# Stick-breaking attention in groups of four heads, and its side projection moved to the delta stage

## The reference

```python
def stick_breaking(q, k, v, q_pos, k_pos):
    z = einsum('bqhd,bkhd->bhqk', q, k) * HEAD_DIM ** -0.5
    visible = k_pos[None, :] < q_pos[:, None]
    log_keep = where(visible, log_sigmoid(-z), 0.0)
    later = cumsum(log_keep, axis=3, reverse=True) - log_keep
    w = where(visible, exp(log_sigmoid(z) + later), 0.0)
    return einsum('bhqk,bkhd->bqhd', w, v)

def mixer_output(h, o_a, o_b, o_c, z, g_post, w_out):
    o = concatenate([o_a, o_b, o_c], axis=-1) * silu(z)
    return h + rmsnorm(einsum('btm,md->btd', o, w_out), g_post)
```

## Time and profile before

| | us |
|---|---|
| runs, median (lowest to highest) | 2085.74 (2085.29 to 2086.71) |
| profiled execution, span of the page | 2087.2 |
| PE busy | 1956.1 |
| DVE busy | 824.0 |
| ACT busy | 759.4 |
| POOL busy | 499.1 |

### The profile page before, as it was taken

How to read it: one execution, slowest core, us unless ns; L and a number is a source line. 1 busy time by engine, 2 the same in 40 slices (tenths; PEclk the granted TensorE clock), 3 DMA queues, 4 the chain that set the end, 5 groups by cost and what they waited for, 6 DMA issues and landing times. The chain is left out here.

```text
span 2087.2 us, 25680 instructions
## 1 busy us (share of the span) xinstructions
PE 1956.1 (94%) x9682; PEld 1222.7 (59%) x9682; DVE 824.0 (39%) x1596; ACT 759.4 (36%) x1590; POOL 499.1 (24%) x436
## 2 busy tenths in 40 slices
PE   6989993999999999999989998999999999969997
PEld 6944441666666666666645554555555555647775
DVE  5723432223222222222216775444454444553332
ACT  4413541222222222222214443344344444455564
POOL 0004312123222231223100000233332333324433
PEclk9999996999999999999998998999999999989999
DMA  4210204100000111102001112000100000165562
GB/s 127 95 32 10 65 1 27 32 27 32 21 32 27 62 57 37 32 27 67 21 28 45 41 41 73 11 21 17 61 28 11 21 7 11 39 180 155 168 191 89
DMA packets 120887, 108.13 MB, mean 52 GB/s; under 512 B 34337, under 2 KB 96065, under 8 KB 120769
## 3 DMA queue, kind: packets, MB, share of 16 engines
q1 hardware_dynamic: 117616, 95.62, 16.5%
q0 software_dynamic: 3152, 10.91, 1.4%
HBM read 65.54 MB, written 41.08 MB: 51 GB/s over the span
## 5 line engine op out<-in xcount | busy, mean ns | idle before, releaser
L330 PE MATMUL side_acc<-hT,wslot 128*128 128x512 f32 (+1 forms) x1360 | 592.5, 546 | 4.4 <-DMA wslot<-in_w_in 4.4
L1570 DVE TENSOR_TENSOR_SCAN prod<-keepb,prod 128x512 f32<-128x512 f32 (+4 forms) x184 | 208.4, 1133 | 286.8 <-ACT keepb L1509 286.4
L1552 POOL TENSOR_TENSOR beta<-beta,prod 128x512 f32<-128x512 f32 (+4 forms) x184 | 174.9, 951 | 588.0 <-DVE prod L1570 588.0
L330 PEld LDWEIGHTS side_acc<-hT,wslot 128*128 128x128 f32 x1360 | 218.3, 192 | 146.0 <-issue 135.6
L1509 ACT ACTIVATE keepb<-b_z 128x512 f32<-128x512 f32 (+4 forms) x184 | 97.7, 531 | 298.4 <-PE b_z L1443 191.2
L460 PE MATMUL acc<-hT,wslot 128*128 128x512 f32 (+1 forms) x480 | 180.6, 532 | 5.4 <-DMA wslot<-in_w_in 5.4
L1440 PE MATMUL b_z<-reg 64*128 64x512 f32 (+3 forms) x360 | 179.9, 580 | 4.8 <-PEq L1793 4.8
L724 POOL TENSOR_TENSOR atl<-at,cf 128x512 f32<-128x512 f32 x102 | 139.8, 1404 | 173.0 <-DVE at L944 173.0
L964 DVE TENSOR_TENSOR xt<-xt,b_kq 128x512 f32<-128x512 f32 x85 | 58.4, 688 | 303.5 <-PE b_kq L791 303.5
L1467 PE MATMUL b_o<-wt,vrow 128*64 128x128 f32 x1232 | 173.4, 280 | 0.5 <-DVE wt L1584 0.5
L1467 PEld LDWEIGHTS b_o<-wt,vrow 128*64 128x64 f32 x1232 | 129.5, 136 | 35.2 <-issue 33.7
(11 more groups left out here) (197 smaller groups left out, 2773.6 us busy)
## 6 DMA issues: line engine op xcount, KB each, us to landing
uT_scratch<-side_stage SPq DMA_DIRECT2D x36, 256.0 KB, 2.0
hT<-mix_scratch SPq DMA_DIRECT2D x17, 512.0 KB, 6.7
hT<-sz_scratch SPq DMA_DIRECT2D x17, 512.0 KB, 8.1
sz_scratch<-side_stage SPq DMA_DIRECT2D x32, 256.0 KB, 2.0
reg<-in_x_prompt SPq DMA_DIRECT2D x15, 512.0 KB
wslot<-in_w_in SPq DMA_DIRECT2D x15, 512.0 KB, 4.0
xres<-in_x_prompt SPq DMA_DIRECT2D x15, 512.0 KB
out_y_prompt<-yy POOLq DMA_DIRECT2D x15, 512.0 KB, 6.4
```

Source lines behind the costliest of these rows:

```text
L330: last = pe.matmul(self.acc[:, n % 2, 0:width], wslot[:, t % 2, k, :], hT[:, k, c0:c0 + width], start=(k == 0), stop=(k == KT - 1))
L1552: pool.tensor_tensor(w, w, prod[0:R, rowno[s] % 2, k0 + 1:k0 + nk + 1], ALU.mult).then_inc(w_ready, 1)
L1570: dve.tensor_tensor_scan(prod[0:R, row % 2, k0:k0 + nk][:, ::-1], kv, kv, prod[0:R, row % 2, k0 + nk:k0 + nk + 1], ALU.mult, ALU.bypass).t ...
```

## The change

Three things change together.

- All eight z tiles are projected raw in the delta stage (RAWZ = KT = 8): 17 tiles, 680 pieces. POINTS has 38 slots per token tile. The output stage takes the sigmoid of eight z tiles and multiplies it with z.
- The stick-breaking stage has no side projection. Its unit is a group: one query tile, up to 512 keys, four heads; there are 46. Each head has its own PSUM bank of scores. The two heads of a pair stand next to each other, on the array's two row halves in the scores and, tile by tile in turn, on its two column halves in the value products. The scan's start value is carried over by a small copy per group; keepb and beta lie in `hT`, which the stage no longer reads.
- The order of loads and stores: the spill and reload of two blocks and the loads of `w_out` stand at the start of SP's queue, the cache loads between them; blocks 3 and 4 of the output are stored at the end.

```diff
-RAWZ = 4
+RAWZ = KT
-                POINTS = [4, 2, 2, 2] + [2, 1, 1] + [2, 2, 1] * 3 + [0]
+                POINTS = [4, 3, 3, 2] + [3, 1, 2] + [3, 2, 2] * 2 + [3, 2, 1] + [0]
...
-                        for s in range(N + 4):
-                            if s < N:
-                                scores(s)
-                                side.products(pe, side_piece(s), side_piece(s + 1) - side_piece(s))
-                                if 0 <= s - (N - TAIL) < GROUPS:
-                                    turn_keys(s - (N - TAIL))
...
-                            if 3 <= s < N + 3:
-                                turn(s - 3)
-                            if s >= 4:
-                                values(s - 4)
+                        for g in range(G + 2):
+                            if g < G:
+                                scores(g, 0)
+                                scores(g, 1)
+                            if g >= 2:
+                                values(g - 2)
+                            if 1 <= g <= G:
+                                for h in range(BH):
+                                    turn(g - 1, h)
+                            if g == 1:
+                                turn_cache()
+                            if KEY0 <= g < KEY0 + KEYS:
+                                turn_keys(g - KEY0)
...
+                        def turn(g, h):
+                            R = rows_of(groups[g][0])
+                            i = number["weights", g, h]
+                            pe.wait_ge(w_ready, BH * g + h + 1)
+                            free_bank(i)
...
+                        def free_bank(i):
+                            if i >= 2:
+                                wait_kept(pe, i - 2)
...
+                            for h in heads:
+                                half = slice((h % 2) * CH, (h % 2) * CH + CH)
+                                pe.matmul(b_z[:, h, 0:nk], reg[half, QS + pair, q0:q0 + R], reg[half, KS + pair, k0:k0 + nk],
+                                          start=not masks, stop=True, skip_group_check=True).then_inc(z_ready, 1)
...
+                            for pair in range(2):
+                                for h in (2 * pair, 2 * pair + 1):
+                                    wait_kept(pe, number["weights", g, h])
+                                for t in range(nt):
+                                    for h in (2 * pair, 2 * pair + 1):
+                                        v, part, at = key_tiles(g, h)[t]
+                                        last = pe.matmul(b_o[(h % 2) * CH:(h % 2) * CH + CH, pair, 0:R], v,
+                                                         wt[part, g % 2, h, t, 0:R], start=(first and t == 0), stop=(last_ and t == nt - 1))
...
+                        for g in range(G + 2):
+                            if g < G:
+                                carry(g)
+                                for h in range(BH):
+                                    scan(g, h)
+                            if g >= 2 and groups[g - 2][4]:
+                                keep_out(g - 2)
+                            if 1 <= g <= G:
+                                keep(g - 1, 0)
+                                keep(g - 1, 2)
+                            if g == 1:
+                                keep_cache()
...
-        stage(stick_breaking, z_tiles[RAWZ:])
+        stage(stick_breaking)
```

More of the change, by code:

```diff
@@ L1328, in stick_breaking @@
[L1328 to L1337, removed]
@@ L1356, in rows_of, with wait_kept, key_tiles @@
+                number = {item[0:3]: i for i, item in enumerate(ITEMS)}
+                owner = [item[3] for item in ITEMS]
+                kept_by = [owner[0:i + 1].count(owner[i]) for i in range(len(ITEMS))]
+                def wait_kept(eng, i):
+                    eng.wait_ge(kept_act if owner[i] == "act" else kept_dve, kept_by[i])
                 def rows_of(m):
                     return NSAMP if m == TILES else P
-                def key_tiles(s):
-                    m, h, k0, nk = steps[s][:4]
+                def key_tiles(g, h):
+                    m, k0, nk = groups[g][:3]
@@ L1419, in _, with scores @@
                     def _(pe):
-                        def scores(s):
-                            m, h, k0, nk, first, last_ = steps[s]
+                        def scores(g, pair):
+                            m, k0, nk, first, last_ = groups[g]
                             R = rows_of(m)
-                            half = slice((h % 2) * CH, (h % 2) * CH + CH)
-                            if first and h == 0 and m % 4 == 0 and SWAPPED <= m // 4 < NBLK:
+                            q0 = SROW if m == TILES else m * P
+                            heads = (2 * pair, 2 * pair + 1)
+                            if first and pair == 0 and m % 4 == 0 and SWAPPED <= m // 4 < NBLK:
@@ new lines, in turn_keys, with values @@
+                        def turn_keys(n):
+                            i = number["keys", n, 0]
+                            free_bank(i)
+                            for m in key_group(n):
+                                for a in range(2):
+                                    last = pe.transpose(b_w[:, i % 2, 2 * (m % 2) + a, :], reg[:, KS + a, m * P:(m + 1) * P], ident)
+                            last.then_inc(wt_ready, 1)
+                        def values(g):
+                            m, k0, nk, first, last_ = groups[g]
+                            R = rows_of(m)
+                            nt = len(key_tiles(g, 0))
+                            if first and m:
+                                pe.wait_ge(o_kept, m)
+                            for pair in range(2):
[6 more added lines that the diff above has]
+                                                         wt[part, g % 2, h, t, 0:R], start=(first and t == 0), stop=(last_ and t == nt - 1))
+                            last.then_inc(o_ready, 1)
@@ L1557, in _, with carry @@
                     def _(dve):
[L1558 to L1560 removed]
+                        def carry(g):
+                            m, k0, nk, first, last_ = groups[g]
+                            R = rows_of(m)
+                            if g >= 2:
+                                dve.wait_ge(w_ready, BH * (g - 1))
+                            edge = prod[0:R, g % 2, :, nk:nk + 1]
```

322 lines of the change are left out of this document (148 added, 174 removed).

## The result

Four runs of the changed kernel take 2124.56 us in the median (2121.18 to 2129.28), four of the kernel before beside them 2086.22 (2085.29 to 2089.11): ratio 1.0179, 95% interval 1.0166 to 1.0192. The change costs 38 us, where I had forecast a gain of 60. The profiled execution took 2121.18 us.

The account below looks back on a forecast made before the run. The prediction took TensorE's order to bound the delta and stick-breaking stages. Its sum was 2087.2+113-178+5 = 2027 us of span, a run time of about 2025.5 us; the range holding 8 in 10 was 2000 to 2063.

Parts of the forecast that it names:

- The delta stage: Delta stage: 160 more pieces on a full TensorE add 113 us (97 to 117); tile period from 42.2 to about 49.
- TensorE's work in a group: Stick-breaking stage: scores 2.7, values 2.7, transposes 2.1, together 7.5 us a group against 14.2 before.
- rival A: Stick-breaking stage: the array's halves don't overlap for long records; +68 us, 2094 us in all; chance 0.05.
- The cycle: Stick-breaking stage: a full group takes 8.9 us, through scores, sigmoid, four scans, VectorE's copy, turns 2 and 3.
- rival B: Stick-breaking stage: TensorE's clock falls; 2070 us with a fifth of groups at half clock, 2143 with half; chance 0.08.
- 389: Stick-breaking stage: forecast length in us to its last output copy, -178 against 567.4; bounds about 370 and 420.
- The output stage: Output stage: wider sigmoid and gate product and two late mix blocks add 5 us; bounds 0 and +12.

Follow-up runs that it names:

- kernel 3: The changed kernel with three filler products a group ahead of the third turn and GpSimd's product on the first 128 keys only: 2020.03 us, ratio 0.9682.
- The filler: The changed kernel with three unused fp32 products of 512 columns in TensorE's gap before turn 2 of each group: 2077.87 us, ratio 0.9955.
- kernel 4: The kernel before with only the side projection moved to the delta stage, one-head steps kept: 2095.05 us, ratio 1.0037.
- experiment 5: The changed kernel, value products written head by head: 2124.21 us. The output-stage run, sigmoid and gate on four of eight z tiles, is the next one: 2113.52 us.
- kernel 8: The changed kernel with all four copies of turned weights of a group on ScalarE: 1995.89 us, ratio 0.9565.
- kernel 2: The changed kernel with GpSimd's stick-breaking product cut to the first 128 keys of each head and group: 2063.82 us, ratio 0.9879.

## Why the prediction was wrong

**The delta stage: right.** +106.4 for +113, inside its bounds. Line 751's products, as in the earlier trace rows, give a tile period of (1115.5 - 347.9)/16 = 48.0 us for "about 49":

```profile
L751 PE MATMUL b_dr<-cb x17: 379/379/607, 347.9 to 1115.5; 128*128 128x512 bf16 x17
```

The 7 us by which it came out lower say little. In the experiments, whose delta stage is the changed kernel's, the stick-breaking stage's first product starts between 1399.7 and 1407.6, so +108 to +116.

**TensorE's work in a group: too high.** Forecast 2.7 us of scores and 2.7 of values, 7.5 in all. At full clock the scores of four heads take 1.9 us (1601.28 to 1603.19 in kernel 3) and the 32 value records 1.9 (1614.97 to 1616.87), 59 ns a record: less than my lower bounds of 2.4 and 2.0. One head's scores alone take 1.05, so records on different halves of the array overlap here, and rival A had no ground. With 1.0 us for two turns TensorE has 5.8 us of work a group. That helped nobody, since this was not the bound, and it left TensorE with longer idle time, which is what the clock fell in.

**The cycle: the mechanism was right, two of its terms were mis-sized, and this is the step that failed.** Term by term, forecast and then the cycle shown above: scores to sigmoid 1.16 and 1.96; sigmoid to scan 0.70 and 0.69; four scans 5.14 and 6.32; the output copy, priced apart, 0.32; copy and crossing 0.77 and 0.82; turns 2 and 3 1.07 and 1.73. Together 8.84 and 11.84.
- 1.2 us is contention (6.32 for 5.14). "Four scans at 1.284" took the duration from a step in which the product comes after the scan. The same prediction has GpSimd's products of one head run beside the scans of the next, and never asked what that does to either. The earlier trace rows even had a trace of it: a mean of 596 ns for a 128-key scan. In that trace ten of the twenty have no product of GpSimd beside them and take 484 ns each; the other ten take up to 1.21 us. Narrow products alone give 61 us back.
- 1.5 us is the clock: the way from the scores to the sigmoid (0.80) and turns 2 and 3 (0.66), both priced at full clock. The prediction had a gap of 1.4 us a group and gave rival B 0.08, on the ground that at half clock TensorE has no gap. The trace shows why that is no ground: the clock does come back, but each cycle has a new wait, and the two pieces of TensorE's work that lie on the cycle are the ones right behind it. The filler alone gives 47 us back.
- With both nearly away a full group takes 8.9 us, as forecast, and the stage 377.4 for 389: the rest of the sum stood, 12 us too high.

**Rival B** was the nearest: its version with half of the time at half clock gave 2143. But it is only about half of the cause. The rule cited for it from the Trainium skill, "TensorE: Matmul & The Clock Gate", Part 4 (products in transpose mode don't count as busy), isn't decided here. The filler took idle time away and added ordinary products in one edit. In kernel 4 the transposes of before are there and the idle time isn't, and it had 0.98 between the stage's ends.

**The output stage: +11 for +5**, inside its bounds (0 to +12). The upper bound named GpSimd and VectorE slowing each other, which experiment 5 makes likely for a part of it and doesn't show.

**What I had at hand.** A rule of the Trainium skill that bears on contention was not weighed: "SBUF — State Buffer", section "Who interferes with whom", says that a VectorE instruction with two inputs in SBUF contends with a GpSimd instruction that reads SBUF, and that the contention is an exclusive lock, so that the one that comes second is blocked until the first ends. The scan has two such inputs. The runs agree that they contend, and they look much like a lock: the records of kernel 8 end in turn, and the narrow product of kernel 2 ends just behind the scan beside it. They don't prove that the block is whole. A pair takes 1.96 us, less than 1.28 + 1.09 = 2.37; but records that stand alone overlap at their ends too (the first two scans of the cycle above are 1.28 and 1.26 us long and start 1.21 apart), so that sum is too high for taking turns.

## What to carry to other kernels

A duration is only good for the neighbours that it had in the trace. Where a new order puts work of VectorE and of GpSimd side by side that came one after the other, price both durations again, and the more so when the sum makes them the bound. Where an engine gets a wait in every cycle, look at what comes right behind the wait: if the clock falls in the wait, that work runs at half clock. And the slot behind a long row on one engine is the dearest place for a small copy: here the two copies a group that stood behind VectorE's scans were worth 129 us on ScalarE, and the output copies, 0.4 us each, another 18.

## What the runs showed of the hardware

- fp32 scans of 128x512 on VectorE take 1280 ns with GpSimd silent, 1660 in the mean beside its products for part of the time, 1859 beside them nearly always, and 2.05 us for one that has a product beside it throughout. A scan and a product by turns take 1.96 us. GpSimd's product goes from 1091 to 1861 and up to 2060, a product on VectorE from 693 to 1582.
- Added TensorE work, some 2.7 us in each full group, made the kernel 47 us faster, through a clock of 0.95 in place of 0.79.
- On alternating column halves the 32 value records of a group take 1.9 us, and 2.5 written out head by head.
